# Layer 1's last expert block added by TensorE with a slot-by-token matrix, the other rows reloaded beside it

## The reference, cut to what matters

```python
def grouped_expert_mlp(h, expert, weight, w_gu, w_down):
    ...
    def expert_block(args):
        idx, e = args
        gate, up = jnp.split(h_pad[idx] @ w_gu[e], 2, axis=-1)
        return (jax.nn.silu(gate) * up) @ w_down[e]
    ...
    y = y.reshape(-1, d) * slot_w[:, None]
    return jnp.zeros((n + 1, d), y.dtype).at[slot_tok].add(y)[:n]

def reference(...):
    for layer in range(DEPTH):
        ...
        if last:
            x = x + g2 * hierarchical_moe(hx, *moe_w).reshape(x.shape)
        ...
    return rms_norm(x, final_g)
```

## Time and profile before

| | us |
|---|---|
| median of 3 runs | 2764.14 (2763.9 to 2767.92) |
| the profiled execution | 2762.16 |
| its span, first to last instruction | 2760.3 |
| PE busy in the span | 2655.9 (96%) |
| DVE busy | 1034.0 (37%) |
| ACT busy | 544.5 (20%) |
| POOL busy | 226.9 (8%) |
| share of PE in the chain that ended last | 91% |

### The profile page before, as it was taken

The page is one execution under the profiler, slowest core; times in us unless marked ns, Lnnn a source line. Parts: engine busy times, 40 slices in busy tenths (PEclk is TensorE's granted clock), DMA queues, the critical chain, the costliest instruction groups (busy, mean ns, idle before and its releaser), DMA issues.

```text
span 2760.3 us, 34264 instructions
## 1 busy us (share of the span) xinstructions
PE 2655.9 (96%) x13616; PEld 1341.8 (49%) x13616; DVE 1034.0 (37%) x2424; ACT 544.5 (20%) x1138; POOL 226.9 (8%) x341
## 2 busy tenths in 40 slices
PE   6999999999989999999999799899999899999995
PEld 3444456556745544433333354477755444444442
DVE  3221337007736642222222362377746511111114
ACT  3211111117811100000000130288721000000001
POOL 0011200003011110000000000000011000000000
PEclk9999999999999999999999999999999999999998
DMA  9641110206060289999998820300030699999995
GB/s 360 252 185 34 35 42 24 72 0 120 2 239 24 91 321 428 427 399 398 415 393 349 329 73 11 68 2 2 2 140 31 265 405 421 423 423 421 424 408 219
DMA packets 97481, 598.77 MB, mean 217 GB/s; under 512 B 17480, under 2 KB 20768, under 8 KB 72360
## 3 DMA queue, kind: packets, MB, share of 16 engines
q1 hardware_dynamic: 83208, 545.15, 50.3%
q0 software_dynamic: 14112, 51.39, 4.6%
HBM read 554.45 MB, written 42.31 MB: 216 GB/s over the span
## 4 chain that ended last, share of the span: by engine, by line
PE 91%; DMA 4%; DVE 3%; issue 1%; SPq 0%; ACT 0%; POOL 0%; PEld 0%; PEldq 0%; DVEq 0%; POOLq 0%; ACTq 0%
PE PS L1819 36%; PE PS L940 24%; PE PS L1477 8%; PE PS L1290 4%; PE PS L1302 4%; PE PS L1313 4%; PE PS L1824 2%; PE PS L584 1%; PE PS L1829 1%; PE PS L1452 1%; PE PS L1496 1%; DMA ar<-in_x_dram 1%; DMA h2d<-ar 1%; DMA ar<-in_ada_w_dram 1%; PE PS L912 1%
## 5 line engine op out<-in xcount | busy, mean ns | idle before, releaser
L1819 PE MATMUL PS<-ar 128*32 128x512 f32 (+2 forms) x4608 | 1029.6, 594 | 8.7 <-issue 2.9
L1819 PEld LDWEIGHTS PS<-ar 128*32 128x32 f32 (+2 forms) x4608 | 379.1, 138 | 621.2 <-issue 612.9
L940 PE MATMUL PS<-ar 128*128 128x512 f32 (+1 forms) x1600 | 674.9, 578 | 0.7 <-ACT ar L735 0.7
L940 PEld LDWEIGHTS PS<-ar 128*128 128x128 f32 x1600 | 299.1, 190 | 331.4 <-issue 325.7
L1477 PE MATMUL PS<-ar 128*128 128x512 f32 x576 | 256.5, 599 | 0.6 <-DVEq L421 0.6
L1943 ACT ACTIVATE ar<-PS 128x512 f32<-128x512 f32 x49 | 29.3, 597 | 1066.2 <-PE PS L1819 1066.2
L1344 DVE CUSTOM_DVE_ANT_0 ar<-PS,ar 128x640 f32<-128x640 f32 (+2 forms) x208 | 158.0, 797 | 204.0 <-POOL ar L1260 133.5
L1477 PEld LDWEIGHTS PS<-ar 128*128 128x128 f32 x576 | 107.8, 192 | 124.2 <-issue 123.3
L1399 ACT ACTIVATE ar<-ar 128x641 f32<-128x641 f32 (+4 forms) x208 | 159.5, 772 | 0.8 <-DVE ar L1344 0.8
L2036 DVE TENSOR_TENSOR ar<-PS,ar 128x1024 f32<-128x1024 f32 x49 | 60.0, 1225 | 250.4 <-PE PS L1819 145.2
L2013 DVE TENSOR_TENSOR ar<-PS,ar 128x512 f32<-128x512 f32 x49 | 33.9, 692 | 313.0 <-ACT ar L1943 313.0
(11 more groups left out here) (240 smaller groups left out, 1824.0 us busy)
## 6 DMA issues: line engine op xcount, KB each, us to landing
ar<-in_expert_w_gu_dram SPq DMA_DIRECT2D x128, 2048.0 KB, 11.8
ar<-in_expert_w_down_dram SPq DMA_DIRECT2D x64, 2048.0 KB, 11.6
ar<-in_ada_w_dram SPq DMA_DIRECT2D x24, 2048.0 KB, 13.1
ar<-yd SPq DMA_DIRECT2D x36, 512.0 KB, 7.3
ar<-in_ab_w_in_dram SPq DMA_DIRECT2D x7, 2048.0 KB, 8.8
h2d<-ar SPq DMA_DIRECT2D x18, 512.0 KB, 2.6
ar<-in_swa_w_in_dram SPq DMA_DIRECT2D x3, 2048.0 KB, 8.3
ar<-mod SPq DMA_DIRECT2D x3, 1536.0 KB, 7.8
```

What stands on the lines that cost most here:

```text
L940: mm = nc.tensor.matmul(out_, lhs, rhs, start=(k == 0), stop=(k == KC - 1))
L1819: mm = nc.tensor.matmul(out[at:to], lhsT[:, at:to], w[:, k, cols], start=start, stop=stop)
```

## The change: what it does

- `moe_blocks`: layer 1's last two whole blocks (ranks 30 and 31) go to the end. The order is then W W P W P W W P W W P W P W W P W W P W W P W W, blocks 0 to 23.
- The last block's result isn't scattered. DVE leaves it in `yb[1]` (g2 included). `last_hot` builds `hot` on DVE behind result(11): for each token tile a matrix of 128 tokens by 128 slots with the token's weight where the slot is its own. `hot_turned` turns it on PE (8 transposes) behind turn_gu(22), DVE copies it to `hotT`. `final_pe` multiplies `hotT` with `yb[1]`, 2 products of 512 columns for each of 8 tiles, into the banks in which the diagonal products of tiles 2 to 7 are summed; tiles 0 and 1 get the new products alone there. The rows of `yd` that the last block would have filled are filled with zeros at the start (one memset of DVE, one scatter of POOL).
- PE's order at the end is up(22), down(21), turn_gu(22), the 8 transposes, down(22), the overflow test, gate(23), up(23), turn_gu(23), down(23). ACT's and DVE's follow.
- The pieces of block 23 may lie in buffers 3 to 5 alone, those of block 22 in 0 to 2 alone. The order of the pieces is as before.
- When block 22's rows have landed, SP loads the rows of `yd` for tiles 0 to 5 into SLOT1, and those of tiles 6 and 7 behind gate(23) into buffer 5. DVE combines tiles 0 and 1 ahead of result(23).
- `final_pe` starts when result(23) is done. The scaled rows are written over x, and stored from there; `outb` is gone, and so is the meeting of the engines ahead of the final stage.

```diff
@@ -86,9 +86,11 @@
...
+    end = rest[len(rest) - 2 * l:]
+    rest = rest[:len(rest) - 2 * l]
...
-    return seq
+    return seq + end
...
@@ -267,13 +269,15 @@
...
+        last_gate = SLOT0 + 8192
+        hot = gsel.rearrange("p (t n) -> p t n", t=XT)
+        hotT = R(TR + 6144, D).rearrange("p (t n) -> p t n", t=XT)
         yg = [[[R(SLOT1 + 2048 * i + 1024 * j, D) for j in range(2)] for i in range(3)],
-              [[R(a + 1024 * j, D) for j in range(2)] for a in [SLOT0 + 2048 * (i + 1) for i in range(5)] + [SLOT1 + 2048 * i for i in range(3)]]]
+              [[R(a + 1024 * j, D) for j in range(2)] for a in [SLOT1 + 2048 * i for i in range(6)] + [last_gate, last_gate + 2048]]]
...
-        outb = [R(SLOT0 + 1024 * i, D) for i in range(2)]
...
@@ -342,7 +346,8 @@
...
-                    q = min(range(6), key=lambda q: (free_at(q), q))
+                    late = nb - x["last"] if l == 1 else 0
+                    q = min(range(3, 6) if late == 1 else range(3) if late == 2 else range(6), key=lambda q: (free_at(q), q))
                     self.fills[q] += 1
                     x.update(buf=q, fill=self.fills[q], freed=held[q])
...
@@ -367,6 +372,11 @@
...
+        n_out = [n_blk[0], n_blk[1] - 1]
+        share(("{}",), "tab_zero", "hot", 2)
+        share(("{}",), "core_x", "hot_tr", NT)
+        share(("{}",), "tab_in0", "hot_in", 128)
+        share(("{}",), "tab_in1", "yd_zero", 128)
...
@@ -1889,30 +1899,11 @@
...
-                pe.wait_ge(*done(f"{n}_y", nb))
+                pe.wait_ge(*done(f"{n}_y", n_out[l]))
...
@@ -1931,7 +1922,44 @@
...
                 down_product(0, [(R(piece_at[2], 4096).rearrange("p (k n) -> p k n", k=4), 0, P)]).then_inc(S(f"{o}_pe"), 1)
+                if l == 1:
+                    pe.wait_ge(*done(f"{o}_y", b + 1))
+
+            running(6)
+            turn(0)
+            running(1, bank=2)
+            for b in range(n_out[l]):
+                gate(b)
+                if b == 0:
+                    route_shift(pe, l)
+                if b >= 1:
+                    turn_gu(b - 1)
+                if b + 1 < nb:
+                    turn(b + 1)
+                up(b)
+                if b >= 1:
+                    down(b - 1)
+            if l == 0:
+                turn_gu(nb - 1)
+                down(nb - 1)
+                ada_late_product(pe)
+                overflow(pe, l, block, first)
+                return
+            turn_gu(nb - 2)
+            hot_turned(pe, nb)
+            down(nb - 2)
             overflow(pe, l, block, first)
+            gate(nb - 1)
+            up(nb - 1)
+            turn_gu(nb - 1)
+            down(nb - 1)
+
+        def hot_turned(pe, nb):
+            pe.wait_ge(*done("hot", 1))
+            pe.wait_ge(*done("m1_hbT", nb))
+            for t in range(XT):
+                tr = nc.tensor.transpose(PS[:, t // 4, (t % 4) * P:(t % 4 + 1) * P], hot[:, t, :], ident)
+            tr.then_inc(S("hot_tr"), 1)
...
@@ -1941,7 +1969,7 @@
...
-            for b in range(nb):
+            for b in range(n_out[l]):
                 silu(b)
...
@@ -1950,23 +1978,25 @@
...
             overflow(act, l, block)
+            if l == 1:
+                silu(nb - 1)
...
             nc.scalar.activation(ssq[:, 15:16], cst[:, C_ONE:C_ONE + 1], ACT.Sqrt)
 
-        ovm = R(SLOT0, NT * EXP).rearrange("p (t e) -> p t e", t=NT)
...
+        ovm = R(SLOT1, NT * EXP).rearrange("p (t e) -> p t e", t=NT)
...
         def overflow_places(dve, l):
...
-            dve.wait_ge(*done(f"{n}_dn", n_blk[l]))
+            dve.wait_ge(*done(f"{n}_dn", n_out[l]))
...
             for j in range(2):
...
                 dve.wait_ge(*done(f"{n}_dn", b + 1))
-                if b >= 2:
-                    dve.wait_ge(*done(f"{n}_yo{b % 2}", 16 * (b // 2)))
+                filled = b // 2 + (b % 2 if l == 1 else 0)
+                if filled:
+                    dve.wait_ge(*done(f"{n}_yo{b % 2}", 16 * filled))
                 V.tensor_tensor(yb[b % 2], down_out, row, ALU.mult).then_inc(S(f"{n}_y"), 1)
...
             route_slots(dve, l)
...
+            if l == 1:
+                V.memset(yb[1], 0.0).then_inc(S("yd_zero"), 1)
             route_rest(dve, l)
-            for b in range(1, nb):
+            for b in range(1, n_out[l]):
                 gu_in(b - 1)
                 if b + 1 < nb:
                     rows_in(b + 1)
                 mul(b)
                 result(b - 1)
-            gu_in(nb - 1)
-            result(nb - 1)
+                if l == 1 and b == nb // 2:
+                    last_hot(dve, moe.blocks[nb - 1]["parts"][0][0])
             if l == 0:
+                gu_in(nb - 1)
+                result(nb - 1)
                 ada_late_evict(dve)
 
             o = f"v{l}"
@@ -2075,7 +2110,37 @@
                 for q in range(2):
                     dve.wait_ge(*done(f"{n}_yo{q}", 16 * len(range(q, nb, 2))))
                 overflow_places(dve, l)
+            if l == 1:
+                gu_in(nb - 2)
+                dve.wait_ge(*done("hot_tr", 1))
+                V.tensor_copy(hotT.rearrange("p t n -> p (t n)"), PS[:, 0:2, :].rearrange("p b n -> p (b n)")).then_inc(S("hot_in"), 1)
+                result(nb - 2)
             overflow(dve, l, block, first)
+            if l == 1:
+                combine = cmb_tile(dve, 1)
+                mul(nb - 1)
+                gu_in(nb - 1)
+                for t in range(XT):
+                    if t not in ON_PE:
+                        combine(t)
+                result(nb - 1)
+
+        def last_hot(dve, r):
+            ch = chain(dve)
+            V = nc.vector
+            e, eq0, eq1, at, more = t2[:, 24:25], t1[:, 8:8 + XT], t1[:, 16:16 + XT], t2[:, 0:XT], t2[:, 8:8 + XT]
+            ch(V.tensor_scalar(e, ordf[:, r:r + 1], -100.0, None, ALU.add))
+            ch(V.tensor_scalar(eq0, ej[:, 0, 0:XT], e, None, ALU.is_equal))
+            ch(V.tensor_scalar(eq1, ej[:, 1, 0:XT], e, None, ALU.is_equal))
+            ch(V.scalar_tensor_tensor(out=at, in0=rj[:, 0, 0:XT], scalar=1.0, in1=eq0, op0=ALU.add, op1=ALU.mult))
+            ch(V.scalar_tensor_tensor(out=more, in0=rj[:, 1, 0:XT], scalar=1.0, in1=eq1, op0=ALU.add, op1=ALU.mult))
+            ch(V.scalar_tensor_tensor(out=at, in0=at, scalar=-1.0, in1=more, op0=ALU.add, op1=ALU.add))
+            ch(V.tensor_tensor(eq0, eq0, wgt[:, 0, 0:XT], ALU.mult))
+            ch(V.tensor_tensor(eq1, eq1, wgt[:, 1, 0:XT], ALU.mult))
+            ch(V.tensor_tensor(eq0, eq0, eq1, ALU.add))
+            for t in range(XT):
+                last = V.tensor_scalar(hot[:, t, :], cst[:, C_SL:C_SL + P], at[:, t:t + 1], eq0[:, t:t + 1], ALU.is_equal, ALU.mult)
+            last.then_inc(S("hot"), 1)
 
         def moe_pool(pool, l):
             moe, n = Moe(l), f"m{l}"
@@ -2101,9 +2166,14 @@
             pool.wait_ge(*done(f"r{l}_idx", 1))
             for b in range(2, nb):
                 gather(b)
+                if l == 1 and b == 3:
+                    pool.wait_ge(*done("yd_zero", 1))
+                    c = moe.blocks[nb - 1]["col"]
+                    pool.indirect_dma_start(out=yd, out_offset=bass.IndirectOffsetOnAxis(ap=dst_i[:, c:c + 1], axis=0),
+                                            in_=yb[1], in_offset=None).then_inc(S("m1_yo1"), 16)
                 if b >= 4:
                     scatter(b - 4)
-            for b in range(nb - 4, nb):
+            for b in range(nb - 4, n_out[l]):
...
@@ -2143,7 +2213,7 @@
...
-            sp.wait_ge(*done(f"{n}_dn", n_blk[l]))
+            sp.wait_ge(*done(f"{n}_dn", n_out[l]))
...
             def block(b):
...
         def final_sp(sp):
             y_landed(sp, 1)
             for t in range(XT):
+                if t == 6:
+                    assert piece_at[Moe(1).pieces[Moe(1).at["g", n_blk[1] - 1][0][0]]["buf"]] == last_gate
+                    sp.wait_ge(*done("m1_ga", n_blk[1]))
                 y_load(sp, 1, t)
             for t in range(XT):
                 sp.wait_ge(*done("fin", t + 1))
-                sp.dma_start(out[0, t * P:t * P + P, :], outb[t % 2]).then_inc(S(f"out{t % 2}"), 16)
+                sp.dma_start(out[0, t * P:t * P + P, :], XR[:, t, :]).then_inc(S(f"out{t % 2}"), 16)
             for q in range(2):
                 sp.wait_ge(*done(f"out{q}", 16 * (XT // 2)))
 
...
             def combine(t):
                 y1, y2 = yg[l][t % len(yg[l])]
                 x = XR[:, t, :]
-                if l == 1 and t in ON_PE:
-                    dve.wait_ge(*done("c1_pe", ON_PE.index(t) + 1))
-                    for half in range(2):
-                        c = slice(half * 512, half * 512 + 512)
-                        last = nc.vector.tensor_tensor(x[:, c], x[:, c], PS[:, 2 * (ON_PE.index(t) % 4) + half, :], ALU.add)
-                    last.then_inc(S(f"{n}_x"), 1)
-                    return
                 dve.wait_ge(*done(f"{n}_y{t % len(yg[l])}", 32 * (t // len(yg[l]) + 1)))
```

(45 more changed lines are left out.)

33 lines of the change are left out of this document (6 added, 27 removed).

## The result

The changed kernel is slower: median 2775.9 us of 6 runs (2774.41 to 2779.75) against 2763.45 us of 6 runs of the kernel before (2761.7 to 2767.92). The ratio is 1.0047, 95% interval 1.0037 to 1.0057. The profiled execution took 2776.1 us, its span is 2773.9 us; the prediction had 2777.4 as the median and 2773.6 as the span.

A forecast was written before the change was run, and what follows sets the result against it. PE, 96% busy, and the DMA queue were taken as about equally loaded. Terms up to the last down product's end gave 2729.6 us; 44.0 more made a 2773.6 us span, 13.3 over before; median 2777.4, range 2769 to 2784.

The forecast's parts named there:

- block order: Layer 1, blocks 11 and 12: pair blocks closer together leave DMA time short, PE waits; 3.0 us (0 to 5).
- E21: End of down(21), the down product of block 21; predicted at 2682.8 us, 2679.8 before.
- E22: End of down(22), the down product of block 22; predicted at 2706.0 us, 2701.4 before.
- E23: End of down(23), the last block's down product; predicted at 2729.6 us, 2710.6 before.
- largest term: In front of down(22): its weights, issued behind a piece waiting for down(21), stall PE 12.2 us (11 to 14).
- small edits: The memset, `last_hot` and the additional scatter lie beside other work and cost nothing; under 4 us together without that cover.
- the reserve: Layer 1: how far weight pieces land ahead of use; the tightest 6 to 7 us ahead in the kernel before.
- the walk: Rule-based tracing of 96 weight pieces' issue and landing at 427 GB/s; gate and up 3.4 us late at block 12.
- The clock: At down(22): after PE's stall the granted clock is half, so 5 records lose 2.1 us (0 to 3.4).
- The overflow test at nothing: On PE behind down(22): the sequencer runs 4.4 us ahead and hides the test; 0 us (to 1).
- The last block and the final stage: After down(22): block 23 in the open takes 23.6 us, then the final stage, paced by PE's products, 44.0 us.
- The rival with d30 in time: At down(22): its weights arrive in time, the new order costs nothing; 4.0 us faster than before, median 2760.1; chance 7%.

The follow-up runs named there:

- eight kernels: The changed kernel, the kernel before with only the new block order, and six built on the changed kernel; result(0) to result(21) took 468.81 to 470.58 us.
- the run with three dense places: Kernel before with layer 1 reordered so that four pair blocks stand with one whole block between two of them; 2765.38 us in one execution.

## Why the prediction was right

| step | predicted | measured |
|---|---|---|
| memset, `last_hot`, zero scatter | 0 | 0 |
| block order | 3.0 | 0.9 (0.2 to 1.9 in eight kernels) |
| E21 | 2682.8 | 2681.5 |
| E21 to the start of down(22) | 14.2 | 14.9 |
| down(22), clock's part of it | 9.0, 2.1 | 9.6, 2.5 |
| E22 | 2706.0 | 2706.0 |
| E22 to E23 | 23.6 | 23.9 |
| E23 to the end | 44.0 | 44.0 |
| span | 2773.6 | 2773.9 |

**The largest term held, and its mechanism was tested.** u31, d30 and d31 were issued within 3.3 us of down(21)'s end, PE stood once, in front of down(22), and the clock was at half at the end of it. With d30 ahead of u31 the wait is gone, with d30 behind d31 it is 4.7 us longer. PE's idle time of 13.34 us counts from the end of the transposes, 1.6 us behind E21; my 12.2 counted from E21 + 2.0. The landing itself is 0.6 us later than my value, and down(22) starts another 0.1 behind it, so the term is 0.7 long. The landing took 12.89 us from the issue of d30, where 7.6 to 8.4 and 5.0, less the 1.1 us between the two issues, would be 11.5 to 12.3. That is within the 1.2 us that scatter(21) could add. It was mis-sized by 0.7, not misplaced.

**The small edits at nothing** held: the memset and the zero scatter moved nothing, and `last_hot` runs on DVE behind result(11) and is done at 2463.7 us (4.1 us of work, where I had estimated 3.5), with 2.13 us of idleness left ahead of the next gu_in.

**The block order was mis-sized: 3.0 predicted, 0.9 measured.** The direction and the place (block 12, by a g or u piece) were right, and the run with three dense places bears out the reserve. The step that failed is the size of the reserve that the walk gave: it had PE waiting 3.4 us at block 12, and the eight kernels waited 0 to 1.7. I can't say which of the walk's rules made it too small. The rate is the one that I had varied (1.3 us at 433 GB/s), but in after the stage moved 426 GB/s on average with the pieces waiting in the queue (median 18.7 us to land; 11.3 and 12.2 before), and that is the walk's 427. With three dense places the waits of 2.08 and 2.62 us fit neither 427 nor 434 GB/s. The walk is good to 2 or 3 us a place, and its cause of error stays open. E21 came 1.7 us later than before, but 0.8 of that was there at result(0) already, in front of the changed stage.

**The clock was mis-sized by 0.4: 2.1 predicted, 2.5 measured** (9.64 us for down(22), against 7.12 with d30 ahead and 7.09 in the run in which PE was kept busy). The other 0.2 us of that row are the product itself, which I had at 6.9 and which takes 7.1 at full clock. I had taken its length from two cold stretches of the kernel before; d30 last gives 1.4 in the same place. A size to half a us wasn't to be had.

The last two misses, +0.7 and +0.6, and the order's -2.1 with 0.8 us of shift at the start of the stage cancel at E22. The agreement there, to 0.1 us, is luck; the large terms are good to 0.6 to 2.1 us each.

**The overflow test at nothing** held: down(22), gate(23) and up(23) stand in the timeline as one group of 48 records without a gap.

**The last block and the final stage** held. PE stood 1.41 and 0.78 us around turn_gu(23), down(23) took 7.13 us, the 80 records went from 2731.32 to 2765.89, 34.6 us against 34.3, and from their end to the end of the span are 8.0 us against 8.3. The 1.47 us of idleness in front of them didn't lower the clock, as I had written. No wait of DVE on a store is left. The rows of `yd` were issued 4.9 us after E22, as taken from the earlier trace rows.

**The rival with d30 in time** was priced right as well. It gave a span of 2756.3; the kernel that makes it true has 2758.1, and the slow records of down(23) make 1.5 of the 1.8 us between them. So the change without its late piece is worth about 2 us of span: 5.6 gained behind E23, 3.6 lost between result(21) and result(23), where the last block now stands in the open (34.4 us against 30.8; 1.5 of it are those slow records). In the medians it can't be told from nothing.

## What to carry to other kernels

When an edit restricts where a buffer may lie or what runs last, write down the end of each in-order DMA queue: which issue waits for which release, and what is queued behind it. A piece whose own buffer is free for over 20 us is still late if it stands behind one whose buffer isn't; exchanging two entries of the list was worth 14 us here, while the part of the change that was meant to gain was worth 2. Work taken out of a final stage pays when it is put where PE waits anyway, and the loads behind it must be traced to their landing first.
